# A decode step's compression: gathered pages turned in place by VectorE instead of TensorE, and two attention units moved into the last projection tile

## The reference, cut to what matters

```python
past_c = pool_c[page_table].reshape(Bd, PAST_LEN, 2, N_KV_HEADS, HEAD_DIM)   # 16 pages of 128 rows each
# compress(): rows -> chunks of 16 rows, both halves m of a block of 32
ch = rows[:, :n_chunk * 16].reshape(B, n_chunk, 16, N_KV_HEADS, HEAD_DIM)
for m in range(2):
    hid = hid + (einsum('bnshd,sdf->bnhf', ch, w1p[m]) + const)[:, m:m + n_cmp]
kc_or_vc = einsum('bnhf,fd->bnhd', gelu(hid), w2)
```

## Time and profile before

| | us |
|---|---|
| median of three runs | 2148.2 (2145.26 to 2151.51) |
| the profiled execution | 2153.62 |
| its span | 2151.8 |
| TensorE busy in the span | 2076.7 (97%) |
| VectorE, ScalarE, GpSimd busy | 1050.8, 621.8, 634.2 |
| the last projection tile (line 972) | 13.7, from 163.4 to 177.1 |

### The profile page before, as it was taken

How to read it: one execution, slowest core, us unless ns; L and a number is a source line. 1 busy time by engine, 2 the same in 40 slices (tenths; PEclk the granted TensorE clock), 3 DMA queues, 4 the chain that set the end, 5 groups by cost and what they waited for, 6 DMA issues and landing times.

```text
span 2151.8 us, 28977 instructions
## 1 busy us (share of the span) xinstructions
PE 2076.7 (97%) x10068; PEld 1303.7 (61%) x10068; DVE 1050.8 (49%) x2141; ACT 621.8 (29%) x1326; POOL 634.2 (29%) x782
## 2 busy tenths in 40 slices
PE   7998999999999999999999999999999999999997
PEld 5454665678778888888886556544444444444442
DVE  3225888753477685354444558623332323232334
ACT  1124777655335561111111221011111111111114
POOL 0002655301000000000000000266666666666562
PEclk9998999999999999999999999999999999999998
DMA  8202000246331111122213116699999999999966
GB/s 240 104 0 109 2 2 2 87 189 246 131 79 40 33 27 41 34 65 79 79 40 124 59 49 241 251 369 366 357 355 346 357 367 340 336 359 366 358 168 236
DMA packets 145601, 378.35 MB, mean 176 GB/s; under 512 B 28339, under 2 KB 94599, under 8 KB 120779
## 3 DMA queue, kind: packets, MB, share of 16 engines
q1 hardware_dynamic: 117507, 291.67, 36.7%
q0 software_dynamic: 27120, 84.40, 13.5%
q10 hardware_dynamic: 864, 0.79, 0.2%
HBM read 342.53 MB, written 58.00 MB: 186 GB/s over the span
## 4 chain that ended last, share of the span: by engine, by line
PE 76%; SPq 6%; DVE 5%; DMA 5%; issue 4%; ACT 3%; DVEq 0%; ACTq 0%
PE PS L1332 19%; PE PS L1562 14%; PE PS L1573 7%; PE PS L972 5%; PE PS L1471 5%; SPq L750 4%; PE PS L861 4%; DMA arena<-in_w_exp_down 3%; PE PS L1455 3%; PE PS L1005 2%; PE PS L1042 2%; PE PS L1147 2%; PE PS L866 2%; SPq L758 2%; PE PS L1633 2%
## 5 line engine op out<-in xcount | busy, mean ns | idle before, releaser
L1332 PE MATMUL PS<-arena 128*128 128x258 f32 x2352 | 514.7, 381 | 2.9 <-DVE arena L2453 2.7
L1332 PEld LDWEIGHTS PS<-arena 128*128 128x128 f32 x2352 | 445.6, 190 | 70.1 <-issue 3.1
L1562 PE MATMUL PS<-arena 128*128 128x512 f32 x1040 | 459.7, 595 | 11.9 <-DMA arena<-in_w_exp_down 7.0
L1659 ACT ACTIVATE arena<-PS 128x258 f32<-128x258 f32 (+12 forms) x525 | 237.3, 464 | 656.6 <-PE PS L1332 238.1
L1562 PEld LDWEIGHTS PS<-arena 128*128 128x128 f32 x1040 | 192.7, 190 | 254.6 <-issue 239.9
L2833 POOL DMA_INDIRECT arena<-x_rows,tokall x276 | 277.5, 1005 | 166.4 <-DVE tokall L2684 96.5
L1573 PE MATMUL PS<-arena 128*128 128x512 f32 x520 | 233.9, 592 | 0.5 <-ACT arena L1659 0.5
L2817 POOL MEMSET arena<- 128x2 f32 x1 | 0.1, 100 | 739.7 <-PE PS L1471 739.7
L2703 DVE TENSOR_TENSOR arena<-PS,arena 128x256 f32<-128x256 f32 x65 | 27.6, 425 | 327.3 <-ACT arena L2000 180.5
L1573 PEld LDWEIGHTS PS<-arena 128*128 128x128 f32 x520 | 96.4, 191 | 109.2 <-issue 108.6
L2697 DVE STREAM_TRANSPOSE arena<-arena 128x1024 f32<-128x1024 f32 x67 | 135.7, 2026 | 43.9 <-DMA arena<-x_rows,tokall 43.4
(11 more groups left out here) (344 smaller groups left out, 2265.7 us busy)
## 6 DMA issues: line engine op xcount, KB each, us to landing
arena<-in_w_exp_down SPq DMA_DIRECT2D x65, 1024.0 KB
arena<-in_w_exp_gate SPq DMA_DIRECT2D x55, 1024.0 KB
arena<-in_w_exp_up SPq DMA_DIRECT2D x55, 1024.0 KB
arena<-in_w_in SPq DMA_DIRECT2D x34, 512.0 KB, 5.3
expert_rows<-arena SPq DMA_DIRECT2D x16, 512.0 KB
arena<-in_w_exp_gate SPq DMA_DIRECT2D x10, 768.0 KB
arena<-in_w_exp_up SPq DMA_DIRECT2D x10, 768.0 KB
arena<-in_x_prompt SPq DMA_DIRECT2D x9, 512.0 KB
```

Source lines behind the costliest of these rows:

```text
L1332: ins = mm(PS[:, bank, 0:QT], lhs[:, l0 + k, :], right[:, r0 + k, c0:c0 + QT], start=first and k == 0, stop=k == kh - 1, skip_group_check= ...
L1562: ins = mm(PS[:, 2 + s, :].rearrange("p (h n) -> p h n", h=2), xgT[:, s, k, :], chunk(w, k), start=k == 0, stop=k == KT - 1)
L1659: return fn(out, in_, ACT.Copy)
```

## The change

It does five things.

1. Each page is gathered by four indirect DMAs of 128 descriptors of 4 KB (a quarter chunk: 4 rows) in place of one of 128 x 16 KB; the indices `pgq` come from eight more small loads of the page table. There are four buffers in place of two; page 4 and later wait for `dh_done` of page b - 4.
2. VectorE transposes the page in place, 4 instructions of 128 x 1024 per page in blocks of 32 x 32 (`turn_page`). `cmp_hidden(b)` reads the page itself as the moving operand: 256 columns in 8 runs of 32 neighbouring values. `cmp_turn`, `cmp_take` on both engines and `hTc` are gone, as are half of the window copies on VectorE (ScalarE takes whole banks now). W1 is loaded a second time in the new order of rows (16 loads on SP, during the last projections).
3. Page 0 is transposed in four pieces inside VectorE's last attention steps (k = NU, NU + 2, NU + 4, NU + 6), page 1 right behind attention, page b + 1 in step b. The 32 small copies of `sample_queries` go to ScalarE.
4. The order of the selected gathers becomes 2, 3, 0, 1, 4, 5, 6, 7, with waits on `dh_done`.
5. The last projection tile is taken out of the loop and projected keys first; the scores of unit 0 lie behind its second step, those of unit 1 between its halves, and `cmp_out()` of the prompt moves from tile j = 7 to j = 6. Units 0 and 2 use banks 4 and 5, unit 1 banks 0 and 1, as the projection has 2 and 3. ScalarE and VectorE are reordered to match: exponentials of units 0 and 1 before `tok_T(NT - 1, (2,))`, `rope_keys(NT - 1)` behind the maxima of unit 0, `rope_queries(NT - 1)` behind those of unit 2.

The core of the diff:

```diff
-        cmp_page = [at(PG_A, 16, KV), at(PG_B, 16, KV)]
+        cmp_page = [at(o_, 4, 4 * KV) for o_ in (PG_A, PG_B, PG_E, PG_F)]
...
-            cmp_turn(0, None)
+            pe.wait_ge(s_w1, 31 * 16)
             for b in range(BD):
-                if b + 1 < BD:
-                    cmp_turn(b + 1, b)
+                cmp_hidden(b)
...
+            def cmp_hidden(b):
+
+                W = WIN_AT.get(b, ())
+                rows = cmp_page[b % 4].rearrange("p i (s v g h b) -> p s h v g i b", s=4, v=2, g=2, h=2)
+                pe.wait_ge(turned, NT + 4 * b + 4)
+                if b >= 2:
+                    pe.wait_ge(sem("hid_add"), b)
                 for u in range(8):
+                    kv = u // 4
+                    for p in range(2 * (u % 4), 2 * (u % 4) + 2):
+                        ins = mm(PS[:, 2 + b % 2, kv * 256:(kv + 1) * 256].rearrange("p (g i b) -> p g i b", g=2, i=4),
+                                 W1[:, kv, p, :], rows[:, p // 2, p % 2, kv], start=p == 0, stop=p == 7)
+                    if u in (1, 3, 5) and u // 2 < len(W):
+                        window_turn(W[u // 2])
+                        if u > 1:
+                            window_scores(W[u // 2] - 1)
+                E.do(ins, sem("dh_done"))
...
+            pe.wait_ge(tok_ev, NT - 2)
+            t = ORDER[NT - 1]
+            for c in (1, 0):
+                for k in range(KT):
+                    last = mm(PS[:, 2 + c, :], xT[:, k, t * P:(t + 1) * P], wtb[:, k, c * 512:(c + 1) * 512], start=k == 0, stop=k == KT - 1)
+                    if (c, k) == (1, 1):
+                        scores(0)
+                    if (c, k) in ((1, 3), (1, 6), (0, 3)):
+                        turn_tile(NT - 2, ({(1, 3): 0, (1, 6): 1, (0, 3): 2}[c, k],))
+                E.do(last, tok_mm)
+                if c:
+                    scores(1)
+            turn_tile(NT - 1, (2,))
...
+            def turn_page(b, i):
+
+                if i == 0:
+                    dve.wait_ge(*page_in(b))
+                v = cmp_page[b % 4][:, i, :]
+                E.do(V.transpose(v, v), turned)
+
             for k in range(NU + LAG + 3):
+                if k in (NU, NU + 2, NU + 4, NU + 6):
+                    turn_page(0, (k - NU) // 2)
...
+            sample_queries()
+            for i in range(4):
+                turn_page(1, i)
             for b in range(1, BD):
...
+                for i in range(4):
+                    if b + 1 < BD:
+                        turn_page(b + 1, i)
+                    if i == 0 and b == 5:
+                        window_row()
+                    if i == 1:
+                        hidden_sum(b - 1)
+                    if i == 2 and b == 5:
+                        window_probs()
...
+            def pages_in_four(b):
+
+                for i in range(4):
+                    G.indirect_dma_start(out=cmp_page[b % 4][:, i, :], out_offset=None, in_=a["cmp"].rearrange("n (r s) c -> (n r) (s c)", s=4),
+                                         in_offset=bass.IndirectOffsetOnAxis(ap=pgq[:, 4 * b + i:4 * b + i + 1], axis=0)).then_inc(CMP_IN[b % 4][0], 16)
...
             for b in range(2, BD):
-                pool.wait_ge(sem("ct_done"), PC + ct_at["c", b - 2, 7] + 1)
-                pages(cmp_page[b % 2], a["cmp"], b, sem(f"pg{b % 2}"))
+                if b >= 4:
+                    pool.wait_ge(sem("dh_done"), b - 3)
+                pages_in_four(b)
```

297 lines of the change are left out of this document (123 added, 174 removed).

## The result

| kernel | median us | runs | ratio to before (95%) |
|---|---|---|---|
| before | 2149.42 (2145.11 to 2152.25) | 7 | |
| after | 2137.58 (2134.00 to 2140.03) | 7 | 0.9944 (0.9934 to 0.9955) |

The changed kernel is faster, by 11.8 us (0.56%). The prediction was 2120.0 with a range of 2106 to 2135: the sign is right, the time lies 2.6 us above the range, and the gain is 42% of the 27.9 us that were forecast. The profiled execution of after took 2139.3 us (span 2137.3).

The account below looks back on a forecast made before the run. TensorE was taken to bound the compression and mostly the attention, with VectorE close behind. Compression -24.9, end of attention +6, start of attention -5 and selected branch -4 sum to -27.9 us from 2148.2: 2120 us, range 2106 to 2135.

Parts of the forecast that it names:

- the precedent of 1.8 us per fall: Compression, wait before page 2: a fallen TensorE clock costs 1.8 us more, sized from a loss in the old selected branch.
- rival A: VectorE's page transposes run at one value per cycle, about 1.2 us each; sum -37.5 us, 2111 us; chance 0.18.
- the transpose: VectorE in the compression: each of a page's four transposes takes 2.03 us, 8.1 us per page.
- Removed, 33.7 us: Compression on TensorE: page 0's turning 7.4, seven pages' turning 24.5 and the wait for page 2 1.8 us disappear.
- Clock at the start of the stage, +1.8: Page 0's product at the compression's start: its first 3.6 us run at half clock, costing 1.8 us.
- Moving operand in runs of 32 values, 0: Hidden products of the compression: reading the operand in 8 runs of 32 values costs 0 us.
- rival C: Hidden products at line 1147: the scattered moving operand slows each record, kernel slower than before, 2187 us; chance 0.04.
- End of attention, +6: VectorE's last attention steps: page 0's four transposes cost 1.5 us each, +6 us, bounds 0 and +8.
- Start of attention, -5: First attention units: scores inside the last projection tile bring unit 5 5 us earlier, and that stays; bounds -3 and -9.
- Selected branch, -4: Selected branch: gathers spread over time remove TensorE's wait for page 7 and the clock's fall; -4 us, bounds 0 and -5.
- Rival B: Compression: TensorE waits 0.5 to 1 us at each of pages 3 to 7; 2132 us; chance 0.13 with rival D.
- Rival D: Compression: 4 KB gathers at half of 384 GB/s cut the stage's gain to 20 us; 2128 us; chance 0.13 with rival B.

Follow-up runs that it names:

- gate3: The after kernel, but GpSimd gathers page 3 and later pages only when the window cache has landed; 2130.41 us.
- split_all: The after kernel, but windows 0 to 2 wanted first, the others issued once page 2 landed, 4 KB window packets, hidden sums ahead of transposes; 2121.79 us.
- stride run: The after kernel, but pages 6 and 7 are transposed through a view of values 8 apart; 2139.6 us in one run.
- attn_only: The before kernel with only the attention part of the change (units 0 and 1 inside the last projection tile); 2146.39 us, ratio 0.9991.
- before_again: The before kernel, unchanged, run once more for a second trace; 2149.07 us.

## Why the prediction was wrong, and where it was right

**The step that failed: a transfer without a landing time.** For page 2 the prediction worked out a landing, T + 13, and it landed at T + 13.7. For the 4.2 MB of windows it worked out none and put their wait at nothing, though their first turning stands inside page 2's product: at full clock TensorE would have been there at T + 21, and the windows were in at T + 35. It named "the 6 MB that are in the queues" and 16 us for them, which would have had the windows in ahead of need. With 6.3 MB alone in the queues they were in at T + 20, in gate3, and TensorE did not wait for them. But the text's own four buffers put more into the queues: it has page 3 behind page 2 there, and says that pages 4 to 7 wait for a product that is "20 us ahead of need". Just that lets pages 3, 4 and 5 in too, 12.6 MB by T + 35. Before, page 3 was issued only at 431.6 us, and the windows were in at about 436, T + 20. The packets made it worse: at 1 KB against 4 KB the windows got 89 of 400 GB/s. The sign that the prediction gave for itself, a stage of over 95 us, came.

The cost is 14.4 us until TensorE can go on (12.5 of them seen as a wait, the rest hidden behind the fallen clock ahead of it), and 2.2 us at half clock behind it, for which the precedent of 1.8 us per fall was a fair size. That is more than the 12.4 us by which the stage missed (98.4 for 86), because the 7.0 us forecast for waits ahead of pages 1 and 2, and for a fall of the clock behind them, did not come, while small waits (1.3 us), the clock at the start and the products (7.17 us for the 7.0 taken) add some 3 us again.

**Where the forecast looks better than it was.** The two errors have opposite signs: with the transposes at their right price the prediction's sum was rival A's 2111, and the miss would have been 27 us, not 18. In the same way it is in part luck that split_all, which gives the windows their place, comes out at 2121.8 (forecast 2120) with a stage of 83.2 (forecast 86). With rival A's transposes the same sum has a stage of 79.6, and 2.5 of split_all's 3.6 us over it are the wait for the window's softmax and the clock behind it. The prediction named that risk and put it at 0.

**A term of the wrong size: the transpose.** 2.03 us were taken, from rows at a stride of 8 values; it is 1.16 to 1.24 (stride run: 2.05 with a stride of 8 values). Rival A had this right, and with it page 2 ready at T + 18 (product at T + 19.0), no wait for page 1, and a cheaper end of attention. Its 2111 failed for the same reason as the forecast, since it has the forecast's traffic, and by more. The rule of the Trainium skill on cachelines ("SBUF — State Buffer", Door 1), and the rate of one element per cycle and lane ("Vector Engine (DVE) Microarchitecture Reference", 3.8), agree with the trace: that rate was an estimate of 1.07 us, the rows have 1.16. Two groups of rows that agree with each other weighed more than they should, since both had the stride that the new operation lacks.

**Point by point.**
- Removed, 33.7 us: right, to 1 or 2 us. After's stage of 98.4 less the waits (13.8) and the time lost to the clock (2.4 at the start, 1.7 and 2.2 around the wait) is 78.3, where 110.7 - 33.7 is 77.0.
- Clock at the start of the stage, +1.8: pages 0 and 1 take 16.7 us where 14.3 are two pages at full clock, +2.4.
- Moving operand in runs of 32 values, 0: right. 7.17 us for 32 records, 0.22 each, and the same 7.17 for the last page's 32 contiguous ones in the kernel before; rival C is out.
- End of attention, +6: +2.4 to +2.6 (10.5 us from the last scores to T in place of 8.0 or 7.9). The working was right in form, 4 x (transpose - 0.52): with 1.23 it gives 2.8.
- Start of attention, -5: unit 5 starts at 188.3, 5.9 us earlier than in the earlier trace rows (188.2 to 191.0 over the traces of changed kernels), and the last unit's scores 3.9 us earlier (403.3 for 407.2). Part of the 5.9 is the clock, 0.87 from 182 to 198 us for 0.51 before. The median of attn_only gives 2.4. "That what its work comes earlier stays" was too simple; where the rest is lost inside attention was not looked for.
- Selected branch, -4: 41.5 us became 40.2, and the second trace of before has 41.3. The clock no longer falls, but the 2.4 us wait is still there (2.5): it is page 7's gather, issued at 533.8 us, right behind GpSimd's copy of page 1's values out of the buffer (530.8 to 533.5), as before (545.1 to 547.8, and 548.1). So spreading the earlier gathers did not help it.
- Rival B (a wait at each page): not so; after the hole TensorE has no wait in after's stage. Its number, 2132, was nearest, by another way, which is luck.
- Rival D (gathers of 4 KB at half rate): no; 390 to 410 GB/s.

Against the second trace of before, the stages of after make -1.0 (T) -10.7 (compression) -1.1 (selected branch) = -12.8 us at the 344-wide product; against the first, -2.1 -12.3 -1.4 = -15.8. The medians have -11.8. What stands behind that product varies too, whatever the kernel: from the last product of the experts' first matrices (line 1562, in after 1563) to the end of the span it is 53.9 us in before_again, 57.2 in the first trace of before and 56.7 in after. The first trace of before, from which all terms were taken, was of an execution 4.2 us over its median, and the prediction took that difference for a constant to subtract. Against before_again it is 3.0 us late at the 344-wide product, but only 1.4 at the recurrent branch behind it (606.1 for 604.8 us); most of the rest is that end of the program, 3.3 us.

## What to carry to other kernels

When buffers come free earlier or become more, list every transfer that may now be in flight together, with its bytes and the size of its packets, and work out a landing for each one that somebody waits for, above all for those that the change does not touch. With several queues busy, the one with the small packets loses: 4 KB packets, one line of the program, gave 9.6 us here, and together with issuing the wanted part first and taking the hidden sums out from behind a wait, 15.8. And price an operation by a row with its own access pattern; where none exists, let the two ends be cases of equal standing.

## What the runs showed of the hardware

- Two busy queues took packets one for one at 1, 2 and 4 KB (1081 for 1084, 605 for 607, 547 for 539), so a queue's share was its packet's size. With 16 KB packets it was not so (143 for 1094, twice the bytes).
- SyncE's issuing is held up by packets and by traffic: eight loads of 512 KB took 19.1 us of its time at 1 KB packets in after, 4.5 at 2 KB and 3.8 at 4 KB. At 1 KB with less beside them they took 11.7 us in gate3, and 7.8 in the kernel before.
- A transpose of 128 x 1024 values of 4 bytes costs 1.16 us in a row of them for neighbouring values, 2.05 at a stride of 8 on both sides. A product's moving operand in 8 runs of 32 values costs nothing (7.17 us for 32 records, as contiguous).
- The granted clock at the same place of the same program was 0.66 in one execution and 1.00 in another, and T and the compression were 1.2 and 1.5 us later and longer where it had fallen.
